# Local attention in single steps and equal dense shares in a hybrid encoder layer on eight cores

## The reference

```
h = x @ w_in                                    # q, k, v, z of mixers A and B, gate logits ga, gb
ya = windowed_sink_attention(qa, ka, va, sink)  # 8 heads of 64, 2 kv heads, |t-s| <= 128, ALiBi, sink logit
ya = (ya * silu(za)) @ w_proj_a
qh, kh = axial_rope(rms_norm(qb)), axial_rope(rms_norm(kb))
yb = blockwise_global_attention(qh, kh, vb)     # 8 heads, all 2048 keys
yb = (yb * silu(zb)) @ w_proj_b
y  = (sigmoid(ga + b) * ya + sigmoid(gb + b) * yb) @ w_out
out = layer_norm(DN_ALPHA * x + y, ln_g, ln_b)
```

## Time and profile before

| | us |
|---|---|
| median of three executions | 697.12 |
| fastest of the three | 695.37 |
| the profiled execution | 696.03 |
| its span on the slowest core (core 1) | 694.5 |
| spans of the eight cores | 690.5 to 694.5 |
| busy: TensorE / ScalarE / VectorE / GpSimd | 615.0 / 391.8 / 371.9 / 125.4 |

### The profile page before, as it was taken

How to read it: one execution, slowest core, us unless ns; L and a number is a source line. 1 busy time by engine, 2 the same in 40 slices (tenths; PEclk the granted TensorE clock), 3 DMA queues, 4 the chain that set the end, 5 groups by cost and what they waited for, 6 DMA issues and landing times.

```text
span 694.5 us, 13589 instructions; the slowest of 8 cores (690.5 to 694.5 us)
## 1 busy us (share of the span) xinstructions
PE 615.0 (89%) x4440; PEld 237.7 (34%) x4440; DVE 371.9 (54%) x740; ACT 391.8 (56%) x515; POOL 125.4 (18%) x193
## 2 busy tenths in 40 slices
PE   3799988997989999999699799989897999999991
PEld 1356532332333333333233233333332333344440
DVE  2288833326281626265926626174758253579467
ACT  0156678784866566766356275756674767631210
POOL 3268541010011111001111111001110101112012
PEclk9999999998999999999999899999999999999996
DMA  9969739564046432344672543245674224418403
GB/s 136 148 119 126 87 70 157 87 119 58 1 47 107 61 49 39 41 59 76 79 148 49 97 77 48 40 62 92 127 178 103 50 33 61 62 39 202 63 1 121
DMA packets 26772, 57.60 MB, mean 83 GB/s; under 512 B 3024, under 2 KB 5200, under 8 KB 26448
## 3 DMA queue, kind: packets, MB, share of 16 engines
q0 software_dynamic: 21520, 39.36, 41.7%
q1 hardware_dynamic: 5184, 17.38, 7.8%
HBM read 86.65 MB, written 8.39 MB: 137 GB/s over the span
## 4 chain that ended last, share of the span: by engine, by line
PE 73%; DVE 9%; issue 7%; ACT 5%; DMA 4%; POOL 1%; DVEq 0%; ACTq 0%; POOLq 0%
PE PS L257 73%; ACT PT L266 4%; DMA SZ<-ws 2%; DVE PT L269 2%; DMA XT<-xT 1%; DVE T L272 1%; ACT G L266 1%; DVE D L827 1%; DVE WR L269 1%; DVE G L272 1%; DVE STT L574 1%; DVE TR L816 1%; PE PS L405 1%; DVE QB L272 1%; DVE O L269 0%
## 5 line engine op out<-in xcount | busy, mean ns | idle before, releaser
L266 ACT ACTIVATE PT<-PS 128x1024 bf16<-128x1024 f32 (+1 forms) x304 | 292.1, 1018 | 118.4 <-PE PS L257 116.5
L257 PE MATMUL PS<-XT,WROT 128*128 128x512 bf16 x896 | 224.7, 388 | 7.3 <-DVE G L272 6.3
L257 PEld LDWEIGHTS PS<-XT,WROT 128*128 128x128 bf16 x896 | 79.2, 99 | 127.3 <-issue 53.6
L276 POOL DMA_DIRECT2D WROT<-wg x100 | 53.4, 536 | 321.5 <-PE PS L257 320.0
L257 PE MATMUL PS<-PT,VX 128*64 128x512 bf16 (+3 forms) x688 | 97.8, 370 | 9.9 <-DVE PT L269 8.8
L257 PE MATMUL PS<-QB,KB 64*128 64x512 bf16 x512 | 83.6, 387 | 19.2 <-ACT PT L266 18.8
L272 DVE SCALAR_TENSOR_TENSOR G<-G,PS 128x512 f32<-128x512 f32 x64 | 43.0, 681 | 99.2 <-PE PS L257 82.0
L266 ACT ACTIVATE G<-PS,CVH 128x512 f32<-128x512 f32 x64 | 44.1, 689 | 69.7 <-PE PS L257 66.0
L257 PE MATMUL PS<-SZ,XT 128*128 128x384 bf16 (+1 forms) x256 | 58.2, 373 | 15.6 <-DMA XT<-xT 15.5
L257 PE MATMUL PS<-SZ,WR 128*128 128x512 bf16 x256 | 65.7, 383 | 5.7 <-ACT G L266 3.3
L257 PE MATMUL PS<-WR,T 128*128 128x512 bf16 x256 | 60.7, 380 | 0.3 <-DVE T L269 0.2
(11 more groups left out here) (68 smaller groups left out, 454.9 us busy)
## 6 DMA issues: line engine op xcount, KB each, us to landing
WROT<-wg POOLq DMA_DIRECT2D x100, 256.0 KB, 7.3
T<-x SPq DMA_DIRECT2D x8, 512.0 KB, 4.6
out<-T SPq DMA_DIRECT2D x8, 512.0 KB, 4.2
QB<-x SPq DMA_DIRECT2D x6, 512.0 KB, 7.5
out<-QB SPq DMA_DIRECT2D x6, 512.0 KB, 3.6
SZ<-ws POOLq DMA_DIRECT2D x8, 256.0 KB, 9.3
XT<-xT POOLq DMA_DIRECT2D x2, 1024.0 KB, 9.4
WR<-wo POOLq DMA_DIRECT2D x8, 256.0 KB, 18.2
```

What stands on the lines that cost most here:

```text
L257: s.op("pe", lambda e: e.matmul(out, lhsT=lhsT, rhs=rhs, start=start, stop=stop, skip_group_check=skip), reads=reads, writes=writes)
L266: s.op("act", lambda e: e.activation(out=out, in_=in_, func=func, **kw), reads=reads, writes=writes)
L276: s.op(eng, lambda e: e.dma_start(out=out, in_=in_), reads=reads, writes=writes, dma=True)
```

## The change

`batches` groups by kind: every A step is a batch of its own (an A chunk is three batches), and a B chunk stays 8 pairs. The weights are all 1.0. Nothing else differs; the sums of the softmax are computed by the same `ones` matmuls and VectorE transposes as before.

```diff
         def batches(steps):
             out, i = [], 0
             while i < len(steps):
-                n = 1 if steps[i].last else 2
+                n = 1 if steps[i].kind == "A" else 2
                 out.append(steps[i:i + n])
                 i += n
             return out
...
-        def weight_of(i):
-            bt = all_b[i][1]
-            if len(bt) == 1:
-                return 0.9
-            return 1.5 if i + 1 < len(all_b) and all_b[i + 1][1][0].kind == "A" and bt[-1].last else 1.0
-
-        weights = [weight_of(i) for i in range(len(all_b))]
+        weights = [1.0 for _ in all_b]
```

## The result

The changed kernel took 687.0 us (median) against 696.7 us for the kernel before: a ratio of 0.9861, with a 95% interval of 0.9836 to 0.9885. It is faster by 1.4%, which lies within the 2% that the chances call the same. I had said 693.7 in a range from 681 to 706. A median is of all executions; the ratios leave out the few in which one die of the chip ran longer at a lower clock, which shift a median by at most 0.8 us. The profiled span went from 694.5 to 683.9 us.

A forecast was written before the change was run, and what follows sets the result against it. TensorE, 89% busy, was taken as the bound in attention, so its stalls cost time. Terms -20.6 + 5.8 + 13.6 - 1.6 = -2.8 us gave 693.2 or 694.3, stated as 693.7, range 681 to 706.

The forecast's parts named there:

- the chances: Whole kernel: faster (below 683.2 us) 0.17, within 2% 0.76, slower (above 711.1) 0.07.
- The three terms of the single steps: Attention stage, A chunks: removed wait -20.6 us, added blocks +5.8, late bias multiply +13.6.
- The removed wait: A chunks: TensorE's wait for A2's exp ahead of B1's scores goes; 17.7 us plus 16 x 0.18, 20.6 us removed.
- The blocks: TensorE in A chunks: nine blocks instead of six, 0.12 us each, over 16 chunks: 5.8 us added.
- VectorE's late multiply: Chunk ends: A1's bias multiply comes behind `rec`; waits 22.4 us (A1 20.4, A2 2) against 8.8, 13.6 us added.
- Dense shares: About 15 dense matmuls move from B to A chunks in window 0: 1.6 us gained; other windows nothing.
- the sign of shares that I had not counted: TensorE's waits for G (11.8 us): a change above 4 us would mean shares matter in an uncounted way.
- My rival on the clock: Attention stage: long waits bring more half-clock stretches, about 2.3 us each beyond the wait; 705 to 716 us, chance 0.10.
- up to 8: Clock rival's opposite case: if the long waits go, up to 8 us of half-clock cost come back.
- restarts: A chunks: loss on top of each exp wait, 0.17 to 0.18 us, counted as 16 x 0.18 within the 20.6.

The follow-up runs named there:

- Experiments 4: On the changed kernel, every started local step gets its bias multiply at once behind its exp, ahead of the reciprocal chain: 671.1 us, ratio 0.9638.
- 6: On the changed kernel, the second softmax-sum transpose done twice in the other 16 chunk ends, which no A chunk follows: 688.6 us, ratio 0.9878.
- experiment 5: On the changed kernel, the second softmax-sum transpose on VectorE done twice in the 16 chunk ends that an A chunk follows: 705.7 us, ratio 1.013.
- the other four divisions tried: Unequal weights: the old ones (single steps 691.4 us), pairs without the 1.5 (688.0); with multiply ahead, 0.7 for A steps (677.3) or 0.5 ahead of A chunks (682.2).
- without the 1.5 alone: On the kernel before, pairs kept, the weight of 1.5 ahead of A chunks taken away and 0.9 for singles kept: 688.0 us, ratio 0.9875.
- two different means: Kernel before, old weights: single A steps, 691.4 us; or pairs with the second look-ahead batch started behind an A batch's dense share, 687.9 us.

## Why the prediction was right, and where it was not

The three terms of the single steps came out near their size; their sum alone doesn't make the measured time.

- *The removed wait.* Forecast to about 6 us from 22.7; it is 6.4.
- *The blocks.* Forecast 48 more blocks of 0.12 us. In the timeline of the attention stage the matmuls change their kind 546 times before and 597 times after, 51 more: three per A chunk, and by the order of the code one more at each of the three places where an A chunk follows an A chunk, which I had not counted. The price held. In these rows of the changed kernel a dense block of 8 goes from 411.43 to 413.26, 1.83 us, which is 8 x 0.213 + 0.12, and single scores go to 413.59, 0.33 us:

```profile
411.43 1.90 PE L257 MATMUL PS<-XT,WROT 128*128 128x512 bf16 x8
...
413.26 0.39 PE L257 MATMUL PS<-QA,KA 64*128 64x384 bf16 x4
...
413.59 0.41 PE L257 MATMUL PS<-PT,VX 128*64 128x128 bf16 x4
```

  The price of the earlier trace rows is right; by an estimate from the drain of about 175 ns that the Trainium skill gives ("TensorE: Matmul & The Clock Gate", the latency figures) the block of 8 would have taken 1.88 us, which the trace doesn't bear out.
- *VectorE's late multiply.* Forecast 22.4 us in place of 8.8; it is 23.5. On A1's values it is 18.7 (forecast 20.4), on A2's 2.4 (2.0) and on A0's 2.3 (none); by window 8.7, 2.1, 5.7 and 7.0 us, where 6.8, 4.0, 5.9 and 5.7 were forecast. Experiments 4, 5 and 6 show that the cause is its place behind the reciprocal chain. A0's waits were of a kind that I had missed: the longest, 1.86 us at 165.82, is for a multiply that stands behind O, and O behind the z tile for which `ensure` pumps 12 dense matmuls.
- So the three terms together, -20.6 + 5.8 + 13.6 = -1.2 us, answer to a measured 0 us with equal weights (687.0 against 687.2) and -4.9 with the old ones. The agreement with the first is in part luck. The terms leave out the waits for dense groups (4.3 us less than in the pairs with equal weights) and the clock. By window, single steps took 3.3 us more in window 0 with the old weights and 4.3 more with equal ones, where the terms give no such loss; one chunk of window 2, below, gave 5.6 and 5.4 us back.

What was wrong is the step *Dense shares*, together with a clock taken as unchanged. It gave the equal weights 1.6 us, in window 0, and said of the other windows that "a moved matmul costs what it saved". Measured, equal weights gave 9.1 us on pairs and 4.4 on single steps, and hardly in window 0: from the first to the last O, equal weights on pairs took 0.8, 2.7, 3.2 and 2.5 us less in the four windows, and on single steps window 0 was no shorter (92.8 against 92.5 us). What I left out is, first, the clock: of the spans' 7.8 and 4.5 us, 4.3 and 4.4 are time that TensorE no longer worked at the lower level. Second, each group has a finishing operation on VectorE or ScalarE, for which TensorE's next group but one waits: 4.7 us on pairs, under 1 us on single steps. I had listed waits for G as the sign of shares that I had not counted; they moved by 8.8 us. But shares alone did not move them: single steps with the old weights took them from 11.8 to 3.6 us, equal weights on pairs only to 7.3.

The 3.45 us wait of the earlier trace rows shows both. In the kernel before, VectorE's finishing operations for two projections stood behind a layer normalisation's multiply and the same reciprocal chain that makes the bias multiply late:

```profile
387.47 1.28 DVE L272 SCALAR_TENSOR_TENSOR T<-T,MV,LNG 128x1024 f32<-128x1024 f32 x1
...
389.00 0.26 DVE L823 RECIPROCAL D<-TR 128x16 f32<-128x16 f32 x1
...
390.21 0.71 DVE L830 STREAM_TRANSPOSE R<-D 128x512 f32<-128x512 f32 x1
390.84 1.25 DVE L272 SCALAR_TENSOR_TENSOR G<-G,PS 128x512 f32<-128x512 f32 x2
```

TensorE's next group starts when the first of them is done, at 391.64. From O to O this chunk took 31.7 us in the kernel before, 29.5 with equal weights on pairs (a wait of 2.25 us is left), 26.1 with single steps and the old weights, and 24.1 in the changed kernel, where no wait for G is longer than 0.9 us. So the steps, which shifted the groups against the chain, gave more of it than the weights. The forecast held no such effect of the steps.

The clock gave back 3.2 us averaged over the eight cores. The prediction priced a stretch at 2.3 us from windows that lie 2.1 us too early; TensorE was busy 5.5 and 6.3 us in the true ones, so they cost 2.8 and 3.1 us, and all five together 11 us and not "up to 8". My rival on the clock had its direction wrong for this kernel, but experiment 5 shows that the effect is there: lengthen the waits of the multiply by 0.6 us each and the time at the lower clock more than doubles.

That 687.0 lies in the range is owed to the width of the range: 3 us less were forecast and 9.7 measured, and most of the difference comes from terms that the forecast had put at nothing.

The terms as measured, in the profiled executions: waits for an exp -16.3, their restarts -2.9 (16 x 0.18), for the multiply +14.7, for dense groups -8.8, for O +1.2, blocks +6.1, clock -3.6, the first stage +1.0 (the first O at 113.3 us and not 112.2). That is -8.6 of the -10.6 by which the span fell; 2.0 us are not placed. The restarts and the blocks are counts times the prices of the prediction, not sums of measured times. The two profiles are of different cores, but averaged over the eight cores the listed waits, the clock and the span moved alike (-16.5, +14.7, -8.8, +1.3, -3.2 and -10.6), so the choice of core doesn't explain what is left.

What stays open: why equal shares did as well as or better than the other four divisions tried (without the 1.5 alone, pairs can't be told from equal weights), and why fewer stretches at the lower clock come with them. Less load for VectorE around a chunk end is no explanation, since a smaller share there cost time as well. In the two places followed above a gate group waits for the finishing operation of a projection. That it is a matter of which group falls on which place, with no direction to it, contradicts no row; it was argued, not shown.

## What to carry to other kernels

When a wait has a place, ask what would be late next at that place, on each engine in its own order: here ScalarE's wait of 20 us hid VectorE's, and taking it away by two different means, with the old weights, gave 5 and 8 us. A small operation that TensorE needs must stand ahead of a long chain on its engine, not behind it; moving 16 multiplies by some 2 us in VectorE's order was worth 16 us, more than anything done to the steps or shares. When filler work is redistributed, count its finishing operations and who waits for them, not only its matmuls, and read the granted clock: here it was about half of what equal shares gave on pairs and nearly all on single steps.

## What the hardware showed that I had not expected

Waits for VectorE near 2 us can cost TensorE more than their own length. In the attention stage of the changed kernel the eight cores have 23 stretches at the lower clock. Each began during a wait for a bias multiply of 1.6 to 2.5 us or at most 3.0 us after its end. Not every such wait brings one: on core 6 a wait of 2.3 us and one of 1.8 passed without. With the transposes doubled, 10.1 us of longer waits came with 20 us more at the lower clock and 18.7 us more time. With the multiply ahead, the lower clock in the attention stage is 2.6 us on average, and the mean granted clock of core 6 rises from 0.974 to 0.987:

```profile
core 6: 683.9 us, clock 0.974
```

```profile
core 6: 669.0 us, clock 0.987
```

The cores of one kernel differ in this: of the changed kernel, one core stood 3.4 us at the lower level in the attention stage and five stood 17.1, with spans of 679.9 us and of 681.7 to 683.9 us.
